# Group norm by half rows, and loads moved into and behind the turns of a scan, in a decoder block on one core

## The chip, the cores and the metric

The kernel runs on one core of one Trainium2 chip. The metric is the device time of one execution in microseconds (us); three runs were timed. All data are float32.

## The reference, cut to what matters

One decoder layer on 1024 tokens of width 1024. A combined input projection feeds a short convolution (512 channels) and an RWKV7 recurrence (8 heads of 64), both go through the output projection w_out, and then comes a mixture of experts, top 4 of 32.

```python
p = xn @ w_in
y_conv = c_b * causal_dwconv(c_c * c_h, conv_w)
...
y = rwkv7_scan(r, decay, k, v, -kk, kk * iclr)
mean = jnp.mean(y, axis=-1, keepdims=True)
var = jnp.mean(jnp.square(y - mean), axis=-1, keepdims=True)
y = (y - mean) * lax.rsqrt(var + GN_EPS) * ln_x_w + ln_x_b
y = y + jnp.sum(r * k * r_k, axis=-1, keepdims=True) * v      # the bonus
y_rwkv = y * g                                                # g = sigmoid(d_g) @ w_gate_up
h = x + jnp.concatenate([y_conv, y_rwkv], axis=-1) @ w_out
h = h + moe_ffn(rms_norm(h)); return rms_norm_final(h)
```

The scan's state, and with it y, is linear in v along the index over which the mean is taken (64 values of a head).

## The kernel before, in words

The kernel is written engine by engine (SP issues loads and stores, POOL is GpSimd, ACT ScalarE, DVE VectorE, PE TensorE), each with its own program, tied by semaphores that are waited for by hand. One large SBUF tensor, `arena`, holds nearly everything at fixed places (`at(kb, ...)`, kilobytes from its start), and places are reused from stage to stage. PSUM is one tensor `ps` of 8 banks.

Stages, with times of the profile: input projection and preparation of the scan's inputs `AR` (32 KB from 0), `BK` (32 KB from 32), `V` (from 64) up to about 375 us; convolution, in a loop over RT = 4 channel tiles, up to 412; the scan over NCH = 16 chunks of 64 tokens, two per turn of a loop (8 turns), up to 627; group norm, bonus and gate of y; output projection over TT = 8 token tiles, with residual, norm, router and lists between its halves, up to 795; then 32 experts, whose weights pass through six slots of 2 MB (`wslot`).

What a chunk needs is copied from AR, BK and V to small buffers: `stage` (lines 424, 425, 427) two chunks ahead, once PE has transposed the keys (`s_bt`), and `stage_again` (430) one chunk ahead, once Y is done (`s_y`). The helpers `chunk_half` on each engine name a chunk's steps. On PE, `m_product` (1534) comes one chunk early, `v_transposed` (1543) turns V by a product with the identity, `scores` (1550) begins a chunk's own part, `bk_transposed` (1561) waits for POOL's scaled keys (586); `e_`, `f_` and `ft_product` (1568, 1574, 1580) are the doubling steps of an inverse, `x`, `sa`, `state` and `y` products end it. The code of a turn is about 750 pairs of weight load and matmul. After the loop PE, ACT and DVE run one more half chunk (the drain), whose last step is ACT's copy of Y (832).

Each conv row tile goes to DRAM (`conv_d`, POOL 575) and POOL waits for it to land (577) before the next; the bonus rows went to DRAM earlier (`bonus_d`). After the last convolution row has landed, SP loads the four bonus tiles of 512 KB (437) and the gate weights (438), and then enters the scan's loop.

After the scan, per channel tile i (4 tiles of 128 channels by 1024 tokens), with `centre` = identity minus a block mean: PE `centred(i)` (1736), ACT `square` (867), PE `variance` (1747), ACT logarithm and exponential (881, 884), DVE scales (1207), adds bias and bonus (1212), PE `gate_of` (1754) and DVE multiplies by it (1215, 1216). All is double-buffered by whole tiles; the variance and gate banks are single:

```python
            variance(0)
            gate_of(0)
            for i in range(1, RT):
                variance(i)
                if i + 1 < RT:
                    centred(i + 1)
                gate_of(i)

            pe.wait_ge(s_wo, 16 * (RT + 4))
            pe.wait_ge(s_mix, RT)
```

Then `out_project(t, h)` (1773) multiplies token tile t by half h of w_out's columns, 8 products of 128x512: first the 4 of the convolution's channels, then the 4 of y's. A residual (DVE 1227, 1228), a square sum (ACT 915), a root and the scaled rows (DVE 1258) follow for each tile, and PE transposes them (1820) between the next tile's two halves. w_out's first half (455) is loaded at the end of the scan; the convolution rows (461), w_out's rest (462), constants (463, 464) and the first three expert weight slots (466) when the scan has ended; the router's inputs (468 to 470) and x (474) once the last gate product is done; the other three slots (502) when expert 0's tokens have been gathered.

## Time and profile before

| | us |
|---|---|
| three runs | 2333.19, 2338.95, 2339.39 (median 2338.95) |
| profiled execution, its own time | 2338.62 |
| its span, first to last instruction | 2337.1 |
| scan, first product to last Y copy | 412.19 to 626.62 |
| from there to the output projection's first product | 29.25 |
| mean granted clock of TensorE, share of full speed | 0.99 |

The profile lists, for one execution, each instruction with its start and duration, by engine and line. "Idle before" is the engine's idle time in front of an instruction, and "<-" names what released it; "issue" means that the profile shows nothing it waited for.
### The profile page before, as it was taken

The numbers are of one execution on the slowest core, as the hardware profiler recorded it, in microseconds if no ns is written. First come the engines' busy times: TensorE is split into PE (matmuls) and PEld (weight loads), VectorE is DVE, ScalarE is ACT, GpSimd is POOL, SyncE is SP. The second block draws the span as 40 slices with busy tenths as digits, with TensorE's granted clock in tenths as the row PEclk, the third lists the DMA queues.
The fourth block names the chain that finished last, engine by engine and source line by source line (L and its number), as shares of the span: only waits on it lengthen the run. The fifth ranks groups of instructions, "written<-read, shape, count | busy, mean of one in ns | idle before, by whom it ended". The sixth has DMA issues, their size and how long they took to land.

```text
span 2337.1 us, 46297 instructions
## 1 busy us (share of the span) xinstructions
PE 2283.6 (98%) x18286; PEld 1685.4 (72%) x18287; DVE 773.2 (33%) x1812; ACT 475.8 (20%) x979; POOL 343.8 (15%) x360
## 2 busy tenths in 40 slices
PE   8999999899999999999999999999999999999997
PEld 3444444799744678878887788878887788778875
DVE  6666411454434422222322222222222232223324
ACT  3223000344423211111111111111111111111113
POOL 0000000111102311111111111112111211112112
PEclk9999999999999899999999999999999999999999
DMA  3021111322443467977997779778897799668976
GB/s 139 27 76 40 54 45 54 107 70 78 165 186 110 183 230 276 351 289 266 334 350 283 276 297 344 283 282 315 296 349 276 285 334 350 266 252 333 350 301 255
DMA packets 111409, 534.97 MB, mean 229 GB/s; under 512 B 26771, under 2 KB 60711, under 8 KB 86752
## 3 DMA queue, kind: packets, MB, share of 16 engines
q1 hardware_dynamic: 89200, 489.30, 53.8%
q0 software_dynamic: 22160, 44.98, 7.6%
q8 instruction: 35, 0.57, 0.1%
q14 instruction: 14, 0.11, 0.0%
HBM read 485.24 MB, written 40.05 MB: 225 GB/s over the span
## 4 chain that ended last, share of the span: by engine, by line
PE 93%; DVE 3%; DMA 2%; issue 1%; ACT 1%; POOL 0%; SPq 0%; POOLq 0%; DVEq 0%; ACTq 0%
PE ps L1861 38%; PE ps L1881 18%; PE ps L1417 12%; PE ps L1773 5%; PE ps L1891 2%; PE ps L1870 2%; PE ps L1568 2%; PE ps L1580 2%; PE ps L1464 1%; PE ps L1574 1%; PE ps L1900 1%; DVE arena L1100 1%; PE ps L1550 1%; DMA idx_g<-list_s 1%; PE ps L1669 0%
## 5 line engine op out<-in xcount | busy, mean ns | idle before, releaser
L1861 PEld LDWEIGHTS ps<-arena 128*128 128x128 f32 x7808 | 925.9, 191 | 16.2 <-issue 15.2
L1861 PE MATMUL ps<-arena 128*128 128x128 f32 (+2 forms) x7808 | 926.9, 281 | 1.0 <-ACT arena L933 0.8
L1881 PE MATMUL ps<-arena 128*128 128x512 f32 x1024 | 453.3, 595 | 0.0
L1881 PEld LDWEIGHTS ps<-arena 128*128 128x128 f32 x1024 | 190.2, 190 | 221.3 <-issue 220.5
L1417 PE MATMUL ps<-arena 128*128 128x512 f32 x768 | 334.6, 595 | 0.8 <-ACT arena L739 0.8
L1314 DVE TENSOR_SCALAR arena<-ps,arena 128x160 f32<-128x160 f32 x256 | 98.3, 384 | 615.1 <-PE ps L1861 536.1
L1417 PEld LDWEIGHTS ps<-arena 128*128 128x128 f32 x768 | 146.0, 191 | 188.7 <-issue 188.7
L938 ACT ACTIVATE arena<-arena 128x160 f32<-128x160 f32 x256 | 86.1, 336 | 823.5 <-DVE arena L1314 823.5
L651 POOL DMA_INDIRECT sum_s<-arena,idx_s x31 | 51.5, 1662 | 819.6 <-ACT arena L953 819.6
L1773 PE MATMUL ps<-arena 128*128 128x512 f32 x256 | 112.8, 594 | 1.5 <-DVE arena L1216 1.5
L1318 DVE SCALAR_TENSOR_TENSOR arena<-arena 128x160 f32<-128x160 f32 x256 | 83.3, 325 | 49.7 <-ACT arena L938 49.7
L1315 DVE TENSOR_SCALAR arena<-ps,arena 128x160 f32<-128x160 f32 x256 | 96.2, 376 | 0.1
L635 POOL DMA_INDIRECT arena<-xn_s,idx_g x33 | 36.3, 1101 | 394.7 <-DMA idx_g<-list_s 204.5
L1335 DVE TENSOR_TENSOR arena<-ps,arena 128x512 f32<-128x512 f32 x31 | 21.4, 692 | 205.4 <-PE ps L1881 205.4
L1773 PEld LDWEIGHTS ps<-arena 128*128 128x128 f32 x256 | 47.5, 190 | 57.5 <-issue 57.5
L1321 DVE TENSOR_TENSOR arena<-arena 128x160 f32<-128x160 f32 x256 | 83.2, 325 | 8.8
L930 ACT COPY arena<-ps 128x512 f32<-128x512 f32 x66 | 35.4, 588 | 212.4 <-PE ps L1900 212.4
L1331 DVE TENSOR_TENSOR arena<-ps,arena 128x512 f32<-128x512 f32 x31 | 21.4, 692 | 161.6 <-PE ps L1881 161.6
L953 ACT ACTIVATE arena<-arena,idx_s 128x512 f32<-128x512 f32 x31 | 22.4, 722 | 202.1 <-DVE arena L1335 202.1
L1870 PE MATMUL ps<-arena 128*128 128x160 f32 x384 | 57.5, 299 | 2.7 <-issue 2.7
L1580 PE MATMUL ps<-arena 64*64 64x64 f32 x1328 | 54.3, 221 | 6.0 <-issue 5.4
L1870 PEld LDWEIGHTS ps<-arena 128*128 128x128 f32 x384 | 53.3, 190 | 2.9 <-issue 2.9
(265 smaller groups left out, 1849.0 us busy)
## 6 DMA issues: line engine op xcount, KB each, us to landing
arena<-gu_w SPq DMA_DIRECT2D x128, 2048.0 KB, 13.5
arena<-dn_w SPq DMA_DIRECT2D x64, 2048.0 KB, 14.1
arena<-dn_b SPq DMA_DIRECT2D x32, 512.0 KB, 16.2
arena<-w_in_t SPq DMA_DIRECT2D x26, 512.0 KB, 3.2
arena<-arena SPq DMA_DIRECT2D x50, 256.0 KB, 2.7
arena<-w_out SPq DMA_DIRECT2D x2, 2048.0 KB, 10.8
arena<-x SPq DMA_DIRECT2D x8, 512.0 KB, 5.3
xn_s<-arena SPq DMA_DIRECT2D x8, 512.0 KB, 2.6
```

The source lines that it names most:

```text
L651: pool.indirect_dma_start(acc_d, bass.IndirectOffsetOnAxis(ap=idx_s[:, 0:1], axis=0), Yt, None, compute_op=ALU.add).then_inc(s_sc, 16)
L938: nc.scalar.activation(sgm[f % 2], gt[f % 2], ACT.Sigmoid, scale=ALPHA).then_inc(s_gs, 1)
L1314: nc.vector.tensor_scalar(gt[b], ps[:, b, 0:C], g0, LIMIT, ALU.add, ALU.min).then_inc(s_g1, 1)
L1315: nc.vector.tensor_scalar(lt[b], ps[:, b, C:2 * C], g1, LIMIT + 1, ALU.add, ALU.min).then_inc(s_gd, 1)
L1318: nc.vector.scalar_tensor_tensor(out=lt[b], in0=lt[b], scalar=1 - LIMIT, in1=sgm[b], op0=ALU.max, op1=ALU.mult).then_inc(s_l1, 1)
L1321: nc.vector.tensor_tensor(actT[:, f, :], lt[b], gt[b], ALU.mult).then_inc(s_act, 1)
L1417: last = nc.tensor.matmul(ps[:, bank + h, :], win[:, slot, kt * P:(kt + 1) * P], xnT[:, kt, h * HALF:(h + 1) * HALF], start=kt == 0, stop= ...
L1580: last = nc.tensor.matmul(out_at(s, 1, h, r), Est[s][own(h), r, :], TTst[s][own(h), r, :], start=True, stop=True)
L1773: last = nc.tensor.matmul(ps[:, 2 * (t % 2) + h, :], mixT[:, k, t * P:(t + 1) * P], wo[:, k % RT, h * HALF:(h + 1) * HALF], start=k == 0, ...
L1861: last = nc.tensor.matmul(ps[:, f % 2, k * C:k * C + size], wslot[u][:, kt, o:o + P], xT[:, kt, 0:size], start=kt == 0, stop=kt == KT - 1, ...
L1870: last = nc.tensor.matmul(ps[:, 1, C:2 * C], wslot[3][:, kt, 3 * P:4 * P], xT[:, kt, :], start=False, stop=kt == KT - 1, skip_group_check= ...
L1881: last = nc.tensor.matmul(ps[:, 2 + h, :], actT[:, ft, 0:P], wslot[4 + h][:, ft, :], start=ft == 0, stop=ft == KT - 1)
```

## The change

1. The centring moves from y to v: `v_transposed` multiplies by blocks of `centre` instead of the identity, so that the scan gives y without its mean. The products `centred` go, and ACT and DVE read y from SBUF.
2. The norm is done by eight half tiles: q counts the first token half of the four channel tiles, then the second. Variance and gate products alternate between two banks each.
3. PE's order: the products of token tile 0 of the output projection stand between the variance and gate products; the convolution's part needs no y. Tiles 1 to 3 need only the first token half of y.
4. The bonus tiles are loaded at the end of the first four turns of the scan's loop, one each. POOL doesn't wait for the last convolution row.
5. In the last turn, once the last chunk's copies have landed, the convolution rows go to 32 KB (BK's place), w_out's rest to 53 KB, and the constants to theirs.
6. x's first tile is loaded ahead of the router's inputs; two expert weight slots follow behind x's second tile, and the third slot is loaded with the other three after the gathers.
7. ACT's table for logarithm and exponential is loaded before the scan's loop. PE waits for `centre` before its first product of the scan.

```diff
-        mixT = at(128, 2 * RT, T)
+        mix_conv, mix_y = at(32, RT, T), at(144, RT, T)
...
-        woA, woB = at(80, RT, D), at(176, RT, D)
+        woA, woB = at(80, RT, D), at(53, RT, D)
...
@@ SP
-            sp.wait_ge(s_cvr, RT + 1)
-            for i in range(RT):
-                sp.dma_start(bonus_in[:, i, :], bonus_d[i]).then_inc(s_pi, 16)
-            sp.dma_start(wgate, wgate_d).then_inc(s_pi, 16)
...
-            with sp.Fori(0, NCH // 2 - 1) as it:
+            def stage_turn(it):
                 stage_next(2 * it, 0, 2 * it + 2)
                 stage_next_again(2 * it, 1)
                 stage_next(2 * it + 1, 1, 2 * it + 3)
                 stage_next_again(2 * it + 1, 0)
+
+            with sp.Fori(0, RT) as it:
+                stage_turn(it)
+                sp.dma_start(bonus_in[:, bass.ds(it, 1), :].rearrange("p a t -> p (a t)"),
+                             bonus_d[bass.ds(it, 1)].rearrange("a p t -> (a p) t")).then_inc(s_pi, 16)
+            sp.dma_start(wgate, wgate_d).then_inc(s_pi, 16)
+            sp.wait_ge(s_cvo, 16 * RT)
+            with sp.Fori(RT, NCH // 2 - 1) as it:
+                stage_turn(it)
...
-            sp.wait_ge(s_yc, NCH + 2)
-            sp.wait_ge(s_cvr, RT + 1)
+            sp.wait_ge(s_st[0], 48 * (NCH // 2 + 1))
             for i in range(RT):
-                sp.dma_start(mixT[:, i, :], conv_d[i]).then_inc(s_wo, 16)
-            sp.dma_start(woB, w_out[RW:2 * RW, :].rearrange("(k p) n -> p k n", p=P)).then_inc(s_wo, 16)
...
-            for u in range(3):
-                sp.dma_start(wslot[u], weights_of(0, u)).then_inc(s_wt[u], 16)
+                sp.dma_start(mix_conv[:, i, :], conv_d[i]).then_inc(s_wo, 16)
+            sp.dma_start(woB, w_out[RW:2 * RW, :].rearrange("(k p) n -> p k n", p=P)).then_inc(s_par, 16)
...
             sp.wait_ge(s_gp, 2 * RT)
...
@@ POOL
-            with pool.Fori(0, RT) as i:
+            with pool.Fori(0, RT - 1) as i:
...
+            pool.wait_ge(s_cd, 2 * RT + 1)
+            pool.dma_start(conv_d[RT - 1], conv_st[:, 0, :]).then_inc(s_cvo, 16)
@@ ACT
+            def square(q):
+                i, h = q % RT, q // RT
+                nc.scalar.activation(gn_sq[q], YF[:, i, h * HALF:(h + 1) * HALF], ACT.Square).then_inc(s_ysq, 1)
...
@@ DVE
+            for q in range(2 * RT):
+                i, w = q % RT, slice(q // RT * HALF, (q // RT + 1) * HALF)
+                y = mix_y[:, i, w]
+                dve.wait_ge(s_sd, q + 1)
+                nc.vector.scalar_tensor_tensor(out=y, in0=YF[:, i, w], scalar=prm[:, LNW + i:LNW + i + 1], in1=gn_sd[q],
+                                               op0=ALU.mult, op1=ALU.mult).then_inc(s_nm, 1)
...
@@ PE
-                    last = nc.tensor.matmul(out_at(s, 3, 1 - h, r), Vc[s][own(h), r, :], cst[own(h), K_ID2:K_ID2 + L],
+                    last = nc.tensor.matmul(out_at(s, 3, 1 - h, r), Vc[s][own(h), r, :], centre[own(h), N * h:N * h + N],
                                             start=True, stop=True)
...
+            gate_of(0)
+            gate_of(1)
+            variance(0)
+            pe.wait_ge(s_wo, 16 * (RT + 1))
+            out_part(0, 0, 0, first)
+            variance(1)
+            out_part(0, 0, 0, second)
+            early_group(2)
+            out_part(0, 1, 0, first)
+            early_group(3)
+            out_part(0, 1, 0, second)
+            early_group(4)
+            pe.wait_ge(s_mix, RT)
+            pe.wait_ge(s_par, 2 * 16)
+            out_part(0, 0, 1).then_inc(s_op, 1)
+            early_group(5)
+            out_part(0, 1, 1).then_inc(s_op, 1)
+            early_group(6)
+            early_group(7)
```

(`early_group(q)` is the variance product of half tile q and then its gate product; `out_part(t, h, part, steps)` gives the products of one part of w_out's rows, 0 the convolution's and 1 y's.)

PE's order between the scan's last Y product (L1674) and the transposes of token tile 0 (L1820), before: L1736 is centring, L1747 variance, L1754 gate, L1773 output projection.

```order
L1736 MATMUL ps<-arena,centre 128x512 [waits centre_matrix,post_inputs,Y_copied]
L1736 MATMUL ps<-arena,centre 128x512 x3
L1747 MATMUL ps<-arena,cst 128x512 [waits y_squared] x2
L1754 MATMUL ps<-arena 128x512 x2
L1747 MATMUL ps<-arena,cst 128x512 [waits y_squared,var] x2
L1736 MATMUL ps<-arena,centre 128x512 [waits y_scaled_then_rstd]
```

After, the same place; L1742 is the gate, L1736 the variance, L1747 the output projection.

```order
L1742 MATMUL ps<-arena 128x512 [waits post_inputs,Y_copied]
L1742 MATMUL ps<-arena 128x512
L1736 MATMUL ps<-arena,cst 128x512 [waits y_squared]
L1747 MATMUL ps<-arena 128x512 [waits w_out_in]
L1747 MATMUL ps<-arena 128x512
L1736 MATMUL ps<-arena,cst 128x512 [waits y_squared]
L1747 MATMUL ps<-arena 128x512 x2
L1736 MATMUL ps<-arena,cst 128x512 [waits var,y_squared]
L1742 MATMUL ps<-arena 128x512 [waits mix_ready]
L1747 MATMUL ps<-arena 128x512 x2
```

The centring products are gone, and two products of the output projection stand between one variance product and the next; the pattern goes on to the eighth half tile.

SP's queue from the end of the scan's loop on, before:

```order
L455 DMA arena<-w_out 128x4x1024
L461 DMA arena<-conv_s 128x1024 [waits conv_stage_free,Y_copied]
L461 DMA arena<-conv_s 128x1024 x3
L462 DMA arena<-w_out 128x4x1024
L463 DMA cst<-consts 128x689
L464 DMA entry<-entry 128x320
L466 DMA arena<-gu_w 128x4096 x3
L468 DMA arena<-router_w 128x8x32 [waits gate_product]
L469 DMA arena<-router_b 128x32
L470 DMA arena<-normw 128x1024
L474 DMA arena<-x 128x1024 x2
```

And after:

```order
L459 DMA arena<-w_out 128x4x1024
L464 DMA arena<-conv_s 128x1024 [waits chunk_staged0]
L464 DMA arena<-conv_s 128x1024 x3
L465 DMA arena<-w_out 128x4x1024
L466 DMA cst<-consts 128x689
L467 DMA entry<-entry 128x320
L472 DMA arena<-x 128x1024 [waits gate_product]
L474 DMA arena<-normw 128x1024
L475 DMA arena<-router_w 128x8x32
L476 DMA arena<-router_b 128x32
L472 DMA arena<-x 128x1024
L479 DMA arena<-gu_w 128x4096 x2
```

The wait for the last Y copy is gone from the convolution rows, the expert weights stand behind x's second tile, and there are two of them.

## Rows read from the trace of the kernel before

**Rows 1.** The page: the chain that ended last, shares of the span by engine

```profile
PE 93%; DVE 3%; DMA 2%; issue 1%; ACT 1%; POOL 0%; SPq 0%; POOLq 0%; DVEq 0%; ACTq 0%
```

**Rows 2.** Busy us (PE, PEld, DVE, ACT, POOL) by stretch; then clock, DMA share, GB/s

```profile
412.00:436.00 24.00, 17.73 (x458) 16.94 (x462) 8.60 (x20) 6.57 (x18) 4.65 (x6) 0.86 0.48 160
460.00:484.00 24.00, 24.00 (x756) 23.08 (x754) 11.78 (x27) 11.68 (x32) 4.74 (x6) 1.00 0.28 77
416.00:424.00 8.00, 4.32 (x136) 4.05 (x132) 2.94 (x6) 2.55 (x8) 3.50 (x4) 1.00 0.85 291
426.00:432.00 6.00, 5.61 (x105) 5.61 (x107) 1.69 (x4) 1.48 (x4) 0.00 (x0) 0.50 0.07 20
626.00:650.00 24.00, 20.38 (x51) 8.02 (x47) 11.16 (x14) 15.71 (x22) 2.34 (x4) 1.00 0.95 367
```

**Rows 3.** PE in order of time, 412 to 462: start, duration, line, idle before

```profile
413.56 1.16 PE L1550 MATMUL ps<-arena 64*128 64x128 f32 x16
417.67 0.46 PE L1561 MATMUL ps<-cst,arena 64*128 64x64 f32 x8 [1.58 <-POOL arena L586]
426.39 0.48 PE L1580 MATMUL ps<-arena 64*64 64x64 f32 x4 [4.50 <-issue]
434.46 1.16 PE L1550 MATMUL ps<-arena 64*128 64x128 f32 x16
447.00 0.62 PE L1669 MATMUL ps<-arena 128*64 128x64 f32 x14 [1.05 <-issue]
449.07 1.16 PE L1550 MATMUL ps<-arena 64*128 64x128 f32 x16
461.06 1.16 PE L1550 MATMUL ps<-arena 64*128 64x128 f32 x16
```

**Rows 4.** All engines in order of time, 415 to 417

```profile
415.71 1.78 SPq L437 DMA_DIRECT2D arena<-bonus_s  x4
416.39 1.04 POOL L586 TENSOR_TENSOR arena<-arena,cL 128x512 f32<-128x512 f32 x1 [3.10 <-DMA conv_s<-arena]
```

**Rows 5.** Queue of instruction transfers, in 412:449 and in 461:485: packets, MB, share

```profile
q8 instruction: 5, 0.08, 0.9%
...
q8 instruction: 1, 0.02, 0.2%
```

**Rows 6.** DMA issues (whole run; x in 600 to 700): KB each, median us to landing

```profile
arena<-w_in_t SPq DMA_DIRECT2D x26, 512.0 KB, 3.2
...
arena<-x SPq DMA_DIRECT2D x4, 512.0 KB, 5.6
```

**Rows 7.** 626 to 656: groups by form (busy us, mean ns, idle before); first output product

```profile
L867 ACT ACTIVATE arena<-ps 128x512 f32<-128x512 f32 x8 | 4.8, 597 | 6.6 <-PE ps L1736 6.6
L881 ACT ACTIVATE arena<-ps,gneps 128x512 f32<-128x512 f32 x8 | 5.3, 686 | 1.3 <-PE ps L1747 1.2
L1207 DVE SCALAR_TENSOR_TENSOR arena<-ps,prm_sb,arena 128x512 f32<-128x512 f32 x8 | 5.6, 746 | 13.2 <-ACT arena L884 13.2
L1212 DVE SCALAR_TENSOR_TENSOR arena<-arena,prm_sb 128x1024 f32<-128x1024 f32 x4 | 5.1, 1285 | 0.1
...
655.87 0.67 PE L1773 MATMUL ps<-arena 128*128 128x512 f32 x1 [1.54 <-DVE arena L1216]
```

**Rows 8.** DVE and PE in order of time, 669 to 677

```profile
669.98 0.69 DVE L1227 TENSOR_TENSOR arena<-ps,arena 128x512 f32<-128x512 f32 x1 [13.89 <-PE ps L1773]
...
673.11 1.28 DVE L1258 SCALAR_TENSOR_TENSOR arena<-arena,stat 128x1024 f32<-128x1024 f32 x1
...
676.54 0.71 PE L1820 MATMUL ps<-cst,arena 128*128 128x128 f32 x5
```

**Rows 9.** SP's issues in order of time, 605

```profile
605.50 0.63 SPq L455 DMA_DIRECT2D arena<-w_out  x1
```

**Rows 10.** DVE in order of time in expert 0

```profile
815.72 0.38 DVE L1314 TENSOR_SCALAR arena<-ps,arena 128x160 f32<-128x160 f32 x1 [2.77 <-PE ps L1861]
820.07 0.38 DVE L1314 TENSOR_SCALAR arena<-ps,arena 128x160 f32<-128x160 f32 x1 [2.81 <-PE ps L1861]
```

173 lines of the change are left out of this document (75 added, 98 removed).

## The prediction

> **What bounds the kernel now.** I read the page's chain first: what ended last lies on TensorE (PE) for 93% of the span of 2337.1 us [rows 1]. So a change pays only where PE idles, where its granted clock falls to the lower level, or where it has fewer instructions. The profiled execution took 2338.62 us, 1.52 us more than its span; the median of the three runs is 2338.95 us, 0.33 us above the profiled one, so the sum below is made against 2338.62 and moved by nothing.
>
> The table of windows then shows two places. In the scan, a turn of two chunks takes 24 us with PE fully busy (460 to 484), but in 412 to 436 PE is busy 17.73 us of 24 at a clock of 0.86 [rows 2]. After the scan, in 626 to 650, it is busy 20.38 us of 24 with products of which a third will go [rows 2]. These are the two places that the change touches.
>
> **First turn of the scan.** The score products (L1550) of chunks 0, 1, 2 and 3 start at 413.56, 434.46, 449.07 and 461.06 [rows 3]. So chunk 0 takes 20.90 us, chunk 1 14.61, and from then on a chunk takes 11.99. The excess of chunk 0 is 8.91 us, and three pieces of it can be read [rows 3]. PE waited 1.58 us for POOL's L586, which itself had waited 3.10 us for the last convolution row to land in DRAM [rows 4]. PE stood 4.50 us at "issue", which means that nothing in the profile released it. Then it ran at a clock of 0.50, the 1.2 GHz level, in 426 to 432 [rows 2]: its products take twice their time there: 6 us of them at the lower level cost 3.0 us more than at the upper. Together 9.1, about the 8.91.
>
> The 4.50 us begin at 421.89. Over 416 to 424 the DMA engines are 85% busy [rows 2]: SP has issued the four bonus loads and the gate weights from 415.71 on [rows 4]. The queue of instruction transfers brings five packets in 412 to 449, but one in 461 to 485 [rows 5]. I take this as PE's code of the loop being fetched in its first turn, with one block late behind the bonus loads. In chunk 1, where no bonus load is in the way, the longest such stop is 1.05 us [rows 3].
>
> The change moves the bonus loads to the ends of turns 0 to 3, and POOL no longer waits for the last convolution row. Cost of chunk 0 after: I charge it what chunk 1 costs, 14.61 us, since it too fetches its code beside the staging copies alone. Both chunks then take 29.22 us instead of 35.51: a gain of 6.29. PE now also waits for the centre matrix before its first product, a DVE operation on 128x128 that stands behind the last convolution product as PE's did; a 512-column one takes 0.7 [rows 7], so I put it and its latency at 0.4 us, lost. **Net gain 5.9.** Bounds: if the late code has nothing to do with the loads, only POOL's 1.58 is won, 1.2 net. If chunk 0 has no stop at all it costs 11.99, net 8.5, and if chunk 1 too, 11.1. The row nearest to the case is chunk 1's own.
>
> Each bonus load is issued once per turn behind the copy for the next chunk (L430), and is 512 KB, like a tile of w_in, which lands in 3.2 us [rows 6]. The steady turns use 28% of the DMA engines [rows 2]: nothing added; if it did hold up a copy, that is the fourth rival. ScalarE's table load moves ahead of the scan, where ACT idles behind the convolution: nothing. The product with the centre matrix in V's transposition replaces one with the identity, same shape and count: nothing.
>
> **Between scan and output projection.** The last Y copy ends at 626.62 (the table above) and the output projection starts at 655.87 [rows 7]. In between PE executes 24 products of 128x512: 8 centring, 8 variance, 8 gate. Each costs 0.86 us of PE (24 of L1773 run from 655.87 to the transposes at 676.54 [rows 7, 8]: 20.67/24). That would be 20.6 us of 29.25; the rest is waiting. What ends last is a round through all three: ACT's squares waited 6.6 us for the centring products, and DVE's L1207 13.2 us for ACT's exponential [rows 7], and the next centring product waits for DVE.
>
> After the change the centring products are gone, and 16 of the 24 products that followed at L1773 (tile 0) are laid between the 8 variance and 8 gate products. PE's work from 626.67 to the transposes of tile 0 is thus 8 + 8 + 16 + 8 (tile 1, first half) = 40 products, 40 x 0.86 = 34.4 us, that is 661.1, if it never waits. Does it? Per half, ACT needs a square (0.60), a logarithm (0.69) and an exponential, which I put at the square's size, 0.62: 1.91. DVE needs L1207's 0.75, L1212 at half its 1.285 and some fixed part, 0.70, and a gate product of L1207's kind, 0.70: 2.15 [rows 7]. PE's spacing between variance products is 2.6 to 3.4 us (one of each kind and one or two pieces of the projection), up to 5.1 about the long pieces. So each is fed in time: first half-group scaled from 630.8, mixed at 633.0; the fourth mixed at 641.7, while PE wants it at 642.1; the last mixed at 657.5, which PE's first half of tile 1 doesn't need. I cost PE's waits there at nothing; the cover at the fourth is only 0.4 us.
>
> What is late next is tile 0's norm. DVE can add the residual from 657.5, but x's rows are issued only when the last gate product is done, at 654.3 (before, it was wanted at 669.98 only [rows 8]). A 512 KB load lands 3.2 us (w_in_t) to 5.6 us (x, with others in the queue) after issue [rows 6]: 657.5 to 659.9. From the residual's start to the scaled rows it takes 669.98 to 674.39 [rows 8], 4.41 us: 661.9 to 664.3, with the router's inputs landing at about the same time. I take 663.1 for the transposes, 2 us after PE arrives. Before they started at 676.54 [rows 8]. **Gain 13.4**, with 15.4 (no wait) and 12.2 as ends. After it, PE's order is as before, since each tile costs it the same.
>
> **Loads.** The convolution rows, the second half of w_out and the constants (4.6 MB) move from 626.64 to about 606, behind w_out's first half, issued at 605.50 [rows 9]. At the 367 GB/s of 626 to 650 [rows 2] all 6.7 MB take 18 us: in by 624, before PE wants them at 628. No expert weights compete at 630. The third weight slot is loaded after the gathers instead, at about 801 in the old time. Expert 0 uses up a slot in 8.7 us (DVE reads two results of PE per slot, 4.35 us apart [rows 10]), from some 807 on. Four slots of 2 MB need 5.7 us each at 367 GB/s: the third is in by 808 and wanted at 824, the last by 825 and wanted past 840. Nothing added; if the cover went, some 5 us.
>
> **Sum.** 2338.62 - 5.9 - 13.4 = **2319.3 us**. With every low end of gain 2325.2, with every high end 2312.1.
>
> **Where a page differs.** The Trainium skill, "Runtime: NRT & Kernel Launch", section "Instruction fetch mechanics", says that crossing a code block costs one DMA tail-bump, "mostly hidden". The stops of 1.05 and 4.50 us speak against it [rows 3]; by the rule the 4.50 has another cause and stays, which is the first rival below. The same section calls the instruction memory "only 2 cache lines", with which a loop of this length would be fetched anew in each turn; that is the fourth rival, and the single packet of a later turn speaks against it [rows 5].
>
> **Rivals.**
> - *The late code has another cause* (the entry into the loop, not the loads). For it: the profile names no releaser. Against: the DMA load just then, and stops of only 1 us elsewhere. Gain 1.2 instead of 5.9: 2324.0 us. Chance 0.12.
> - *The new burst delays code at the scan's end.* The loads now fill the DMA engines from 606 to 624, while PE leaves its loop for code it has not run. Against: by then much of it may be there, since the drain is short. Price, as in chunk 0: 4.5 of waiting and 3.0 of lower clock, 2326.8. Chance 0.12.
> - *The half-groups run in series.* If a semaphore's latency adds 0.5 us to each ACT and DVE step, the fourth group comes late, and the four groups behind it wait about 1.2 us each: 2324. Chance 0.12.
> - *The other side: code is fetched in every turn.* Then each of the four bonus loads stops PE as the burst did in chunk 0, 4.5 + 3.0 = 7.5 us, 30 in all, and the time is 2349.3, slower by 0.4%. It decides from 6.6 us per turn on (above 2345.6). For it: the loop's code is long. Against: one packet in 461 to 485 where the first turn had five [rows 5]. Chance 0.02.
> - *The change does less than it says* because router inputs or x's rows come still later (they now share the queue with 4 MB of expert weights issued behind them): each us is a us. 3 to 5 us, 2323. Chance 0.12.
>
> **Numbers.** The forecast has 0.50. The range 2312 to 2329 takes in the bounds of the sum and the values of the first, second, third and fifth rival (2323 to 2326.8), and leaves out the fourth and two mishaps at once. A measurement of this kernel can tell about 0.3%, 7.0 us. All but the other side and a pile of mishaps lie below 2331.9: faster 0.94, same 0.03, slower 0.03.
>
> **What would show it.** Right: L1550 of chunk 1 some 15 us after chunk 0's, and a clock near 1.00 in the first turn; bonus loads between chunks with no gap of PE beside them; no wait of POOL for the last convolution row's transfer; PE without an idle piece over 0.5 us from the last Y copy to the end of tile 1's first half; transposes of tile 0 some 36.5 us after that copy (before 49.9); a wait of about 2 us there for the scaled rows. Wrong: a gap at "issue" in the drain, a clock below 1 in the 30 us after the scan, DVE as releaser of the gate products, or gaps ahead of expert 0's fifth gate product.

## The result, and the profile after

| | before | after |
|---|---|---|
| median of the runs, us | 2338.12 (4 runs, 2333.19 to 2339.39) | 2319.47 (4 runs, 2315.90 to 2321.75) |
| profiled execution, us | 2338.62 | 2320.9 |
| its span, us | 2337.1 | 2319.3 |
| mean granted clock | 0.990 | 0.992 |
| first product of the scan (L1534) starts | 412.19 | 412.31 |
| last copy of Y (L832, now L839) ends | 626.62 | 621.50 |
| transposes of tile 0 (L1820, now L1827) start | 676.54 | 657.62 |

The ratio is 0.9925 with an interval of 0.9911 to 0.9938: three quarters of a per cent faster, or 17.5 us of 2338.12 (the medians differ by 18.65 us). The forecast was 2319.3 us.

The share of the chain by engine hardly moves (against [rows 1]), as it must where the time was taken out of pauses:

```profile
PE 94%; DVE 3%; DMA 2%; issue 1%; ACT 0%; POOL 0%; SPq 0%; POOLq 0%; DVEq 0%; ACTq 0%
```

Busy time by stretch, with the columns of [rows 2]. The first three are the scan's first turn, the two chunks after it and a steady turn; then the last turn with the new burst of loads, and the 24 us from the last copy of Y on:

```profile
412.00:436.00 24.00, 21.75 (x649) 20.44 (x651) 11.29 (x25) 9.84 (x27) 6.31 (x8) 1.00 0.31 90
436.00:460.00 24.00, 22.40 (x643) 21.18 (x639) 10.96 (x24) 9.83 (x27) 3.46 (x5) 0.93 0.24 72
460.00:484.00 24.00, 24.00 (x758) 23.08 (x754) 11.81 (x27) 11.70 (x32) 4.68 (x7) 1.00 0.35 99
600.00:624.00 24.00, 21.65 (x584) 19.09 (x581) 7.64 (x17) 10.17 (x27) 2.95 (x5) 1.00 0.77 297
621.50:645.50 24.00, 23.95 (x56) 10.74 (x57) 13.14 (x18) 12.19 (x20) 2.35 (x4) 1.00 0.08 29
```

In 412 to 436 PE is busy 21.75 us at clock 1.00, where it was 17.73 us at 0.86. From 621.50 on it is busy 23.95 of 24 us, where it was 20.38 of 24 [rows 2].

PE in order of time in the first three chunks, as in [rows 3]: the start of the scan, the score products (L1550) that mark each chunk, and every idle piece at "issue":

```profile
412.31 0.68 PE L1534 MATMUL ps<-arena 64*64 64x64 f32 x16 [1.26 <-DVE arena L1132]
413.69 1.16 PE L1550 MATMUL ps<-arena 64*128 64x128 f32 x16
420.64 0.33 PE L1580 MATMUL ps<-arena 64*64 64x64 f32 x4 [0.21 <-issue]
424.88 0.45 PE L1669 MATMUL ps<-arena 128*64 128x64 f32 x8 [0.15 <-issue]
426.64 1.16 PE L1550 MATMUL ps<-arena 64*128 64x128 f32 x16
430.10 0.34 PE L1561 MATMUL ps<-cst,arena 64*128 64x64 f32 x5 [0.67 <-issue]
434.99 0.50 PE L1580 MATMUL ps<-arena 64*64 64x64 f32 x9 [0.91 <-issue]
440.62 0.62 PE L1669 MATMUL ps<-arena 128*64 128x64 f32 x14 [1.60 <-issue]
443.12 2.08 PE L1550 MATMUL ps<-arena 64*128 64x128 f32 x16
456.06 1.16 PE L1550 MATMUL ps<-arena 64*128 64x128 f32 x16
```

Chunk 0 takes 12.95 us (it took 20.90), chunk 1 16.48 (14.61), chunk 2 12.94 (11.99). The stop of 4.50 us is now 0.21 us, in front of the same four records of L1580 (a float32 product has two records, each with a weight load of its own). Chunk 1 has longer stops than before, and chunk 2 begins at the lower clock: the 16 records of its score products take 2.08 us, not 1.16, and 436 to 460 has 0.93. The three chunks together shrink from 47.50 to 42.37 us.

POOL in order of time at the scan's start. It issues the last convolution row's copy to DRAM and works on (L593 was L586, which had waited 3.10 us [rows 4]):

```profile
412.07 0.53 POOL L584 DMA_DIRECT2D conv_s<-arena  x1 [40.29 <-DVE arena L1132]
412.71 1.06 POOL L593 TENSOR_TENSOR arena<-arena,cL 128x512 f32<-128x512 f32 x1
```

The groups of the norm by form in 621.5 to 657, which answer to [rows 7] (square, logarithm, exponential on ACT; the scaling on DVE). ACT still waits for PE's variance products, and DVE for ACT, but PE no longer waits for either:

```profile
L874 ACT ACTIVATE arena<-arena 128x512 f32<-128x512 f32 x8 | 4.8, 617 | 0.0
L886 ACT ACTIVATE arena<-ps,gneps 128x512 f32<-128x512 f32 x8 | 5.5, 688 | 13.3 <-PE ps L1736 13.3
L888 ACT ACTIVATE arena<-arena 128x512 f32<-128x512 f32 x8 | 5.1, 632 | 0.3
L1210 DVE SCALAR_TENSOR_TENSOR arena<-arena,prm_sb 128x512 f32<-128x512 f32 x8 | 6.0, 751 | 14.4 <-ACT arena L888 14.4
```

The end of the stretch in order of time on SP, DVE and PE: x's rows, the residual, the scaled rows, the transposes (against [rows 8]):

```profile
649.32 0.35 SPq L472 DMA_DIRECT2D arena<-x  x1
...
653.15 0.69 DVE L1224 TENSOR_TENSOR arena<-ps,arena 128x512 f32<-128x512 f32 x1 [0.27 <-DMA arena<-x]
...
656.28 1.28 DVE L1255 SCALAR_TENSOR_TENSOR arena<-arena,stat 128x1024 f32<-128x1024 f32 x1
...
657.62 1.09 PE L1827 MATMUL ps<-cst,arena 128*128 128x128 f32 x8 [1.46 <-DVE arena L1255]
```

From the last copy of Y to these transposes it was 49.92 us and is 36.12. So the account is: 5.1 us won up to the last copy of Y (626.62 to 621.50), 13.8 after it, 1.1 given back later (tile 0's transposes to the end: 1660.6 us before, 1661.7 after). Together 17.8, the difference of the two spans. The 5.1 us are one execution against one; below, the other executions spread this part widely.

What is given back is found in expert 0. Its first product starts 18.86 us earlier than before (787.75 for 806.61). Then PE in order of time, at the first down projection, before and after:

```profile
842.72 1.89 PE L1870 MATMUL ps<-arena 128*128 128x160 f32 x12 [2.69 <-issue]
```

```profile
823.89 3.38 PE L1877 MATMUL ps<-arena 128*128 128x160 f32 x12 [2.73 <-issue]
```

The stop at "issue" was there before, at the same twelve records, and it is no longer than it was. Behind it they now take 3.38 us instead of 1.89: 1.5 us for the lower clock (820 to 832 has 0.86, where 838 to 850 had 1.00). About 0.4 us of that is regained behind it.

### The profile page after: what moved, and what is told of

It is laid out like the page before. It is cut to its first block, busy times and chain, and to the rows that moved or that the text cites. A ratio compares the mean times of both kernels' runs of the same rounds, so it can differ in the third digit from the quotient of the medians.

```text
span 2319.3 us, 46282 instructions
## 1 busy us (share of the span) xinstructions
PE 2273.4 (98%) x18270; PEld 1682.5 (73%) x18271; DVE 774.8 (33%) x1816; ACT 477.6 (21%) x983; POOL 344.3 (15%) x360
## 4 chain that ended last, share of the span: by engine, by line
PE 94%; DVE 3%; DMA 2%; issue 1%; ACT 0%; POOL 0%; SPq 0%; POOLq 0%; DVEq 0%; ACTq 0%
PE ps L1868 39%; PE ps L1888 19%; PE ps L1417 13%; PE ps L1747 4%; PE ps L1898 2%; PE ps L1877 2%; PE ps L1568 2%; PE ps L1580 2%; PE ps L1464 1%; PE ps L1574 1%; PE ps L1907 1%; DVE arena L1104 1%; PE ps L1550 1%; DMA idx_g<-list_s 1%; PE ps L1669 0%
## 5 line engine op out<-in xcount | busy, mean ns | idle before, releaser
L1868 PEld LDWEIGHTS ps<-arena 128*128 128x128 f32 x7808 | 925.9, 191 | 17.4 <-issue 15.3
L1747 PE MATMUL ps<-arena 128*128 128x512 f32 x256 | 113.7, 594 | 0.0
L1747 PEld LDWEIGHTS ps<-arena 128*128 128x128 f32 x256 | 47.6, 190 | 55.2 <-issue 54.7
L1580 PE MATMUL ps<-arena 64*64 64x64 f32 x1328 | 53.3, 218 | 1.7 <-issue 1.1
## 6 DMA issues: line engine op xcount, KB each, us to landing
arena<-gu_w SPq DMA_DIRECT2D x128, 2048.0 KB, 12.1
arena<-dn_w SPq DMA_DIRECT2D x64, 2048.0 KB, 14.5
```

What stands on the lines that cost most here:

```text
L1580: last = nc.tensor.matmul(out_at(s, 1, h, r), Est[s][own(h), r, :], TTst[s][own(h), r, :], start=True, stop=True)
L1747: last = nc.tensor.matmul(ps[:, 2 * (t % 2) + h, :], (mix_conv, mix_y)[part][:, k, t * P:(t + 1) * P], (woA, woB)[part][:, k, h * HALF:(h ...
L1868: last = nc.tensor.matmul(ps[:, f % 2, k * C:k * C + size], wslot[u][:, kt, o:o + P], xT[:, kt, 0:size], start=kt == 0, stop=kt == KT - 1, ...
```

## The experiments

Two questions. In the first turn: is it the loads, POOL's wait or the code itself that stopped PE? Behind the scan: which of the three edits (centring moved, halves, early products of tile 0) is worth how much? My theories were those of the prediction. Each variant's own profiled execution is read by two lengths: the first three chunks (from one score product to the third after it), and "tail", from the last chunk's transposing products (L1561 in before and after) to tile 0's transposes. "First packet" is when, to 0.2 us and counted from the scan's first product, the queue of instruction transfers moves its first packet of 16 KB.

| kernel | chunks 0, 1, 2, us | sum | first packet, us | stop at the four records of L1580 | tail, us |
|---|---|---|---|---|---|
| before | 20.90, 14.61, 11.99 | 47.50 | 11.6 | 4.50 | 68.45 |
| c_centre_only | 17.72, 15.95, 11.99 | 45.66 | 9.8 | 3.00 | 65.70 |
| c_first_turn_as_before | 17.36, 15.22, 11.99 | 44.57 | 9.2 | 2.60 | 54.52 |
| b_bonus_in_turns | 15.40, 16.41, 12.99 | 44.80 | 7.2 | 0.81 | 69.52 |
| a_bonus_ahead | 15.65, 14.68, 11.99 | 42.32 | 7.8 | 2.09 | 54.61 |
| a_pool_waits | 14.14, 15.50, 11.99 | 41.63 | 7.0 | 0.26 | 54.60 |
| the change | 12.95, 16.48, 12.94 | 42.37 | 6.0 | 0.21 | 54.66 |
| the change again (d_change) | 12.39, 15.48, 11.99 | 39.86 | 4.8 | none | 54.49 |
| c_groups_first | 12.34, 15.71, 11.99 | 40.04 | 4.8 | none | 57.66 |
| c_last_groups_early | 12.12, 15.70, 11.99 | 39.81 | 4.8 | none | 53.65 |
| d_last_groups_early | 12.95, 16.22, 12.90 | 42.07 | 5.4 | 0.21 | 53.66 |
| a_late_loads | 12.62, 14.67, 11.99 | 39.28 | 4.8 | none | 64.76 |
| d_extra_loads | 12.93, 16.77, 12.90 | 42.60 | 4.8 | none | 54.46 |
| d_code_shift_96 | 13.54, 12.80, 11.99 | 38.33 | 3.6 | none | 54.77 |

Three profiles have the first turn as before (before, c_centre_only, c_first_turn_as_before): their sums have a mean of 45.91 us. Six have that of the change and no other edit in the scan: their mean is 40.57, from 39.28 to 42.37. So the first turn is worth 5.3 us by the means, and single pairs give 2.2 to 8.2.

### The loads ahead of the loop, and GpSimd's wait

**a_bonus_ahead**, the change with its loads put back:

```diff
-            with sp.Fori(0, RT) as it:
-                stage_turn(it)
-                sp.dma_start(bonus_in[:, bass.ds(it, 1), :].rearrange("p a t -> p (a t)"),
-                             bonus_d[bass.ds(it, 1)].rearrange("a p t -> (a p) t")).then_inc(s_pi, 16)
+            sp.wait_ge(s_cvo, 16 * RT)
+            for i in range(RT):
+                sp.dma_start(bonus_in[:, i, :], bonus_d[i]).then_inc(s_pi, 16)
             sp.dma_start(wgate, wgate_d).then_inc(s_pi, 16)
-            sp.wait_ge(s_cvo, 16 * RT)
-            with sp.Fori(RT, NCH // 2 - 1) as it:
+            with sp.Fori(0, NCH // 2 - 1) as it:
                 stage_turn(it)
```

> The changed kernel with one thing undone: the four bonus tiles and the gate weights are loaded ahead of the scan's loop again. Theory (PE's code of the first turn comes late behind these loads): a stop of PE of 3 to 5 us at "issue" at the same product as in the kernel before (L1580 with 4 of 16 records left), some us at the lower clock behind it, chunk 0 (score product to score product) at 18 to 20 us instead of 12.95, the kernel some 5 to 7 us slower than the changed one, that is 13 us faster than before. Rival (the stop comes with the entry into the loop, and went for another reason, such as POOL's wait): chunk 0 stays at 13 us and the time at that of the changed kernel.

Measured: 2320.36 us, ratio 0.9936 [0.9920, 0.9953]. The stop in front of the same four records is back, at 2.09 us, with the DMA engines 74% busy around it:

```profile
422.59 0.33 PE L1578 MATMUL ps<-arena 64*64 64x64 f32 x4 [2.09 <-issue]
```

```profile
412.00:424.00 12.00, 9.52 (x288) 9.09 (x290) 5.84 (x12) 3.99 (x11) 3.91 (x5) 1.00 0.74 257
```

But the clock stays at 1.00. The three chunks sum to 42.32 us, 1.75 more than the mean of the change's first turn and no more than its longest (42.37), so by themselves the loads cost under half of what I had charged them. My 18 to 20 us for chunk 0 and my 5 to 7 us in the time were both too much.

**a_pool_waits**, the change with GpSimd waiting for the last convolution row again:

```diff
-            with pool.Fori(0, RT - 1) as i:
+            with pool.Fori(0, RT) as i:
...
-            pool.wait_ge(s_cd, 2 * RT + 1)
-            pool.dma_start(conv_d[RT - 1], conv_st[:, 0, :]).then_inc(s_cvo, 16)
```

> The changed kernel with one thing undone: POOL waits for the last convolution row to land before it starts on the scan. If that wait was worth its 1.58 us, chunk 0 takes 14.5 us instead of 12.95 and PE's first transposition of keys (L1561) waits for POOL's L593. If the code's arrival sets chunk 0's pace anyway, the wait takes the place of a stop at "issue" and chunks 0 and 1 together stay at 29.4 us.

One execution: 2318.1 us. PE waits 1.13 us for GpSimd and chunk 0 is 14.14 us, near the 14.5 I expected if the wait is a cost of its own; the sum of the three chunks lies between the change's own two executions.

**b_bonus_in_turns**, the kernel before with the new loop of loads alone:

> The kernel before with one part of the change: the bonus tiles are loaded at the ends of turns 0 to 3 of the scan's loop; POOL still waits for the last convolution row. Theory: the stop of 4.50 us and the spell at the lower clock go, the scan ends 3.5 to 5 us earlier, and nothing else moves, so 2334 us. Rival (entry into the loop): the stop stays, 2338 us.

Measured: 2330.36 us, ratio 0.9978 [0.9968, 0.9988]. The 4.50 us stop is 0.81 us and GpSimd's 1.57 us remain. This is 2.7 us less over three chunks than in the profile of before (1.1 less than the mean of the three such profiles), and 0.22% or 5.1 us by the ratio. The spell at the lower clock did not go, as I had expected, but moved to chunk 2. Its tail is 1.1 us longer than before's, because the first output products run at the lower clock:

```profile
650.90:656.30 5.40, 5.38 (x9) 2.45 (x10) 0.24 (x3) 0.00 (x0) 0.00 (x0) 0.69 1.02 373
```

There before's products had the clock at 1.00 (655.80 to 661.20).

**c_first_turn_as_before** puts both back into the change, that is, both diffs above:

> The changed kernel with both edits of the first turn undone: the bonus and gate loads stand ahead of the loop again, and GpSimd waits for the last convolution row ahead of the loop. What stays is the part behind the scan. Theory (the stop of 4.50 us in before needs the loads, and each of the two undone alone cost nothing because their sum has to pass a point at which the granted clock falls): chunk 0 is 20 to 21 us again, clock 0.8 to 0.9 in the first 24 us, the scan 4 to 6 us longer than in the changed kernel, 2323.5 to 2326. Rival (the 4.5 us stop was a matter of where the code of before's stages stands, or of chance): chunk 0 stays at 14 to 16 us and the time within 1 us of the changed kernel's 2319.5.

Measured: 2323.11 us, ratio 0.9940 [0.9924, 0.9957]. Beside 0.9925 and 0.9921 for the change that is 3.5 to 4.4 us, though the intervals overlap. PE in order of time, the two idle pieces of chunk 0:

```profile
413.26 0.47 PE L1557 MATMUL ps<-cst,arena 64*128 64x64 f32 x8 [1.09 <-POOL arena L589]
...
420.09 0.48 PE L1576 MATMUL ps<-arena 64*64 64x64 f32 x4 [2.60 <-issue]
420.36 1.08 PE L1564 MATMUL ps<-arena 64*64 64x64 f32 x16
```

Behind the stop sixteen records take 1.08 us where they take 0.63 at the upper level: the lower clock is back, as in before. So chunk 0 reads: both edits made 12.1 to 13.0 us (13.5 in d_code_shift_96, which starts at the lower clock), GpSimd's wait alone 14.1 and 15.4, the loads alone 15.7, both 17.4 to 20.9. The four profiles with the loads ahead have the stop at 2.09 to 4.50 us, and the ten without at 0 to 0.81: the loads set its size. In three of those four GpSimd's wait is there too, and in those three PE then ran for a while at the lower clock; with the loads alone it did not. My expectation of 20 to 21 us for chunk 0 was too high, here and in c_centre_only: before's own profiled execution, from which I took it, had the longest stop of the three.

### Where the stops lie: code or data

**d_code_shift_96**, the change with 96 more instructions on PE ahead of the loop:

```diff
             pe.addr_align(FETCH_BLOCK, max_nops=0)
+            for _ in range(96):
+                pe.sem_inc(s_pe_apart, 1)
```

> The changed kernel with 96 extra instructions (increments of a semaphore that nobody reads) in TensorE's program ahead of the scan's loop. Theory (the stops at issue are places at which the next piece of the program is not there yet, and lie at fixed distances in the program): the stops move against the code by 96 instructions, which are 48 products with their weight loads, so three groups of 16 products earlier: the stop at the 9th-last product of L1580 and that at the 14th-last of L1669 are gone from there and stand some 1.5 to 3 us earlier in the chunk, at other lines. Rival (the stops belong to a data or semaphore event, or to the loop's own branch): they stay at L1580 and L1669, with the same counts of products behind them. The time stays within 3 us of the changed kernel.

One execution: 2321.04 us. Chunk 1 in order of time, first of d_change, then of the shifted kernel (whose lines stand two further down, so that L1655 is L1653):

```profile
432.59 0.68 PE L1653 MATMUL ps<-arena 64*64 64x64 f32 x16
433.06 0.68 PE L1580 MATMUL ps<-arena 64*64 64x64 f32 x16
433.53 0.68 PE L1659 MATMUL ps<-arena 64*64 64x64 f32 x16
434.14 0.33 PE L1669 MATMUL ps<-arena 128*64 128x64 f32 x2
435.52 0.62 PE L1669 MATMUL ps<-arena 128*64 128x64 f32 x14 [1.05 <-issue]
```

```profile
439.56 0.28 PE L1655 MATMUL ps<-arena 64*64 64x64 f32 x3
440.34 0.57 PE L1655 MATMUL ps<-arena 64*64 64x64 f32 x13 [0.51 <-issue]
440.74 0.63 PE L1582 MATMUL ps<-arena 64*64 64x64 f32 x16
441.20 0.63 PE L1661 MATMUL ps<-arena 64*64 64x64 f32 x16
441.77 0.69 PE L1671 MATMUL ps<-arena 128*64 128x64 f32 x16
```

The stop stood behind the second record of L1669; now it stands behind the third of L1655. In between lie 13 + 16 + 16 + 2 = 47 records, or 94 instructions with their weight loads, for 96 that were added. The stop belongs to a place in the program, not to a semaphore or a tile. The run has a price of its own: the added instructions run while PE has nothing else, its first product waits 7.71 us and starts at the lower clock, 2.8 us later than in the change's profile; the other stops of the first turn are gone. In one execution I can't tell which of that is the earlier start of fetching.

The other thirteen profiles say the same without any shift. They have 46 stops at "issue" behind the first product of the scan, and each lies at one of five places: behind 244, 368, 491, 615 or 738 records of the scan, which are 123 or 124 records apart (the stop of the shifted kernel lies behind 691, which is 738 less 47). And the instructions can be seen to arrive: in all fourteen, each stop ends 2.3 to 3.4 us after a packet of the queue of instruction transfers has started. For the stop at L1580 with the loads ahead this packet comes 7.8 to 11.6 us after the scan's first product, and the stop ends 2.4 to 2.7 us behind it; without them it comes after 3.6 to 7.2. So the loads make the code late, and late code is what PE stands still for.

**d_extra_loads**, the change with a burst of four loads in each of turns 0 to 3:

```diff
-            with sp.Fori(0, RT) as it:
+            for k in range(2):
+                sp.wait_ge(s_bo[k], 16 * RT // 2)
+            for it in range(RT):
                 stage_turn(it)
...
+                sp.dma_start(bonus_in[:, it, :], bonus_d[it]).then_inc(s_pi, 16)
+                for k in range(3):
+                    sp.dma_start(at(84 + 4 * k, T), x[0:P, :]).then_inc(s_extra, 16)
+                sp.wait_ge(s_extra, 48 * it + 48)
```

> The changed kernel with three more loads of 512 KB (rows of x, into a part of the memory that is free there) behind the bonus load in each of turns 0 to 3, so that each of these turns has a burst of four loads, as before had once ahead of the loop. Theory (code of the loop is fetched in the first turn only): the bursts of turns 1 to 3 stop TensorE nowhere, chunks take 11.99 us each there; only the burst of turn 0, if it meets chunk 1's fetch, can lengthen a stop; 2319 to 2324. Rival 4 of the prediction (code is fetched in every turn): a stop at issue of 2 to 4.5 us in each of the turns 1 to 3 and in part the lower clock, 2326 to 2340.

One execution: 2321.53 us. The turns with bursts 1 and 2 by windows (columns as above):

```profile
460.00:484.00 24.00, 24.00 (x756) 23.08 (x754) 11.88 (x26) 11.61 (x33) 4.67 (x7) 1.00 0.51 165
484.00:508.00 24.00, 24.00 (x758) 23.09 (x754) 11.89 (x26) 11.59 (x33) 4.74 (x6) 1.00 0.51 164
```

The DMA engines are nearly twice as busy as in [rows 2], and PE has no idle piece from 460 to 532, behind the bursts of turns 1 to 3. The queue of instruction transfers moves its last packet of the loop before 484, in this run as in before and after. The loop's code is fetched once.

### The stretch behind the scan

**c_centre_only**, the kernel before without the eight centring products (the transposing copy takes its centred form from the centre matrix, as in the change; groups stay whole tiles):

```diff
-                    last = nc.tensor.matmul(out_at(s, 3, 1 - h, r), Vc[s][own(h), r, :], cst[own(h), K_ID2:K_ID2 + L],
+                    last = nc.tensor.matmul(out_at(s, 3, 1 - h, r), Vc[s][own(h), r, :], centre[own(h), N * h:N * h + N],
...
-                if i + 1 < RT:
-                    centred(i + 1)
```

> The kernel before, changed only in where Y is centred: the eight centring products after the scan go, and the transposing copy of each chunk takes its centred form from the centre matrix; tiles stay whole, the first product of tile 0 still stands behind all groups, loads and first turn stay as before. Theory (the 13.8 us gained after the scan are partly the removal of 8 products of 1024 columns in two halves each, about 7 us of PE time in a chain of rounds): the groups' rounds get shorter by what the centring took in them, 3 to 7 us; time 2328 to 2332 where before is 2335. Rival (the rounds are bound by the chain square, product, Ln, Exp, scale, whole tile, and the centring lay in its gaps): under 1.5 us. The first turn must stay at about 20.9 us for its first chunk in both.

Measured: 2333.93 us, ratio 0.9984 [0.9973, 0.9994]; tail 65.70 us, 2.75 less than before, between my two ranges. PE in order of time, and ahead of it the first thing that ACT does there:

```profile
620.84 1.28 ACT L869 ACT_TABLE_LOAD   x1
...
622.90 1.96 PE L1737 MATMUL ps<-arena,cst 128*128 128x512 f32 x4 [2.49 <-ACT arena L866]
...
630.89 2.99 PE L1744 MATMUL ps<-arena 128*128 128x512 f32 x4 [2.60 <-DVE arena L1216]
...
642.25 3.53 PE L1744 MATMUL ps<-arena 128*128 128x512 f32 x4 [2.52 <-DVE arena L1216]
```

Eight products of 0.86 us are gone, 6.9 us of PE, and only 2.75 us come out: PE now waits in their place, and some products behind a wait run at the lower clock (2.99 and 3.53 us for four records, 1.88 at the upper level; before had one such group, of 3.50). Part of the first wait is ACT's table load of 1.28 us, which the centring products had covered and which the change moves ahead of the scan. So this run understates the centring's part by up to that much.

**c_groups_first**, the change with tile 0's sixteen early products behind the groups instead of between them:

```diff
+            variance(1)
+            for q in range(2, 2 * RT):
+                early_group(q)
             pe.wait_ge(s_wo, 16 * (RT + 1))
             out_part(0, 0, 0, first)
-            variance(1)
             out_part(0, 0, 0, second)
-            early_group(2)
...
             out_part(0, 0, 1).then_inc(s_op, 1)
-            early_group(5)
+            out_part(0, 1, 0, first)
+            out_part(0, 1, 0, second)
             out_part(0, 1, 1).then_inc(s_op, 1)
-            early_group(6)
-            early_group(7)
```

> The changed kernel with TensorE's 16 early products of tile 0 behind the norm's groups instead of between them (half groups, centring in the scan and all loads stay as changed). Theory (the early products fill the gaps of the half groups' rounds): tile 0's transposes come about 4 us later, and the time is 2322 to 2325 where the changed kernel has 2319.5. Rival (the rounds are bound by the chain through ScalarE and VectorE, so that the order on TensorE is worth little, and a plain order lets them run closer together): under 1.5 us later. Sign the other way: the groups end earlier by 3 us or more because their products no longer queue behind output products, and the net is zero.

Measured: 2318.95 us, ratio 0.9922 [0.9906, 0.9939]; tail 57.66 us, 3.0 more than the change. The 2322 to 2325 that I expected did not come. Rounds of half groups in order of time, with PE's waits in them:

```profile
620.37 1.12 PE L1736 MATMUL ps<-arena,cst 128*128 128x512 f32 x2 [1.10 <-ACT arena L874]
622.22 1.12 PE L1742 MATMUL ps<-arena 128*128 128x512 f32 x2 [0.73 <-DVE arena L1216]
...
624.39 1.12 PE L1742 MATMUL ps<-arena 128*128 128x512 f32 x2 [0.19 <-DVE arena L1216]
```

Even without anything between them, half groups run at a round of 2.17 us, of which PE waits 0.19 us: DVE's three steps and PE's two products nearly match. So, taken in this order, 2.75 us of the tail's 13.8 come with the centring, 8.0 with the halves and everything else that changed between the two runs (65.70 to 57.66: the moved loads, the table load of 1.28 us), and 3.0 with the early products. All but 0.1 of the 8.0 us lie ahead of the first output product, and PE, ACT and DVE wait for no load there in either run; still, the halves alone have no run of their own. The whole time does not show the 3.0: the change itself was not run on that chip, and the interval spans 7.7 us. The kernel below is 3.2 us faster on that chip, where the tails differ by 4.0.

**c_last_groups_early** and **d_last_groups_early** are one kernel, the change with the last two half groups ahead of tile 0's last eight products:

```diff
             early_group(5)
-            out_part(0, 1, 1).then_inc(s_op, 1)
             early_group(6)
             early_group(7)
+            out_part(0, 1, 1).then_inc(s_op, 1)
```

> The changed kernel with the last two half groups' products put ahead of the last 8 early products of tile 0. Theory (in the changed kernel the transposes of tile 0 wait 1.46 us for VectorE, which is late because it mixes the last half groups late): that wait goes and the transposes come 0.5 to 1.5 us earlier; 2318 to 2319 where the changed kernel has 2319.5, at the edge of what can be told. Rival (VectorE's work up to the residual of tile 0 is fixed by the x load that lands at 653.15, or the last 8 products now stand at the end and are themselves the last link): no gain, within 0.5 us, or up to 1 us lost.

> The changed kernel itself, run beside the variants on one chip, so that they can be compared with it directly. All theories: ratio to before 0.991 to 0.994. By the theory that the size of the stops in the first turn differs from execution to execution, but not their place, the profiled execution stops at the same products of L1580 (x4, x9) and L1669 (x8, x14) as before, with sizes between 0 and 1.7 us, and the part from the last scan chunk's transposition to tile 0's transposes takes 54.6 us again.

> The changed kernel with the last two half groups' products ahead of the last 8 early products of tile 0, now with more rounds beside the changed kernel. Theory: 53.65 us from the last scan chunk's transposition to tile 0's transposes where the changed kernel has 54.66, so 1.0 us less in the whole, 2315 to 2319 where the changed kernel has 2316 to 2320. Rival (the 1.0 us is given back in the experts, whose start is fixed by something else): no difference within 0.5 us.

d_change came out as expected: its ratio is 0.9921, its tail 54.49 us, and its stops (0.39 to 1.17 us) lie at L1580 x9, at L1669 x14 and, not on my list, at L1561 x5, where the change's first profile had one of 0.67. For the variant, the tail is 53.65 and 53.66 us where the change has 54.66 and 54.49, and PE no longer waits for the scaled rows. The time shows nothing of it: 2315.78 us with a ratio of 0.9903 [0.9886, 0.9919] on one chip, 2316.93 with 0.9924 [0.9911, 0.9938] on another, where the change itself ran at 2313.43 and 0.9921 [0.9907, 0.9934]. Whether the 0.9 us is real in the whole stays open; no version here is shown to beat the change.

### The loads of the last turn

**a_late_loads**, the change with the convolution rows, the second half of w_out and the constants behind the last copy of Y again:

```diff
+            sp.wait_ge(s_yc, NCH + 2)
```

> The changed kernel with one thing undone: the convolution rows, the rest of w_out and the constants are issued when the scan has ended. Theory (the early burst is what lets tile 0's products be laid between the norm's): PE waits for the fourth convolution row ahead of the first product of the output projection, wanted 2.7 us after the last Y copy; issued by 1.8 us and 6 us to land, that is a wait of about 5 us, the rest of w_out coming in its cover, so 4 to 6 us slower than the changed kernel. Rival (the early burst costs as much in late code or contention as it gives): no slower. Expected here: PE's drain between the last loop turn and the last Y copy is as long as in the changed kernel, within 0.3 us.

Measured: 2325.99 us, ratio 0.9962 [0.9948, 0.9977], so about 8.6 us behind the change's 0.9925. PE in order of time:

```profile
630.26 3.62 PE L1748 MATMUL ps<-arena 128*128 128x512 f32 x4 [8.37 <-DMA arena<-conv_s]
```

The early products need the convolution rows at 621.9 and get them at 630.3; then four records take 3.62 us at the lower clock, not 1.88. Both together are the 10.1 us by which the tail grows. I had expected 4 to 6: the slowest of the four rows took 9.8 us from issue to landing, not 6, and the lower clock was not in my sum. From the last chunk's transposing products to the last copy of Y it is 18.53 us here, 18.54 in the change and 18.53 before, so the early burst costs the scan's end nothing. The early products can't do without it; what the moved loads are worth without early products, no run shows.

## Why the prediction was right, and where its parts were off

**Start of the scan.** I charged 0.4 us for the wait for the centre matrix, and it is there: PE idles 1.26 us ahead of the scan's first product, released by DVE, where it idled 0.83 before, so 0.43 us. That this product started only 0.12 us later than before (412.31 for 412.19) is chance, since its start differs by up to 4.6 us between executions for a reason ahead of the scan (last section).

**First turn, 5.9 us (1.2 to 11.1).** The profile of the change gives 5.1 us over three chunks and d_change 7.6, and the means over all profiles 5.3; the step holds. That the first pair came so near to the forecast is in part luck, as the spread of 2.2 to 8.2 shows. Its parts were placed differently. I took chunk 0 at 14.61 us and it was 12.1 to 13.0; I took chunk 1 as unchanged at 14.61 and it was 14.7 to 16.5, as if the delay moved on to where code and the chunks' own copies met (argued, not shown). Chunk 2 at the lower clock (0.95 us more), which four of the fourteen profiles have, I had not considered. The reading that the stop is code held back by the bonus loads is shown from three sides: its place moves with the program (d_code_shift_96), its size with the loads (2.09 to 4.50 us with them ahead, 0 to 0.81 without), and the packet of instructions ahead of its end comes late with the loads (7.8 to 11.6 us after the scan's first product, 3.6 to 7.2 without them).

**The late code has another cause (2324.0).** This falls: the 4.50 us went, and the stops that are left in the change's profile are 0.15 to 1.60 us each. By the Trainium skill, "Runtime: NRT & Kernel Launch", section "Instruction fetch mechanics", a crossing is "mostly hidden". The traces of this first turn disagree (0.15 to 1.60 us each).

**From the scan to tile 0's transposes, 13.4 us (12.2 to 15.4).** Measured 13.8. PE's 40 products without a wait were right: it is busy for 34.60 of the 34.66 us. The fourth half group, whose cover I had put at 0.4 us, was ready at 636.72 and wanted at 637.11. I had PE at the transposes 34.4 us after the copy of Y and it arrived after 34.7 (657.62 less the wait of 1.46). I took x's load at 3.2 to 5.6 us and it took 3.8, from 649.32 to the residual at 653.15, so the wait for the scaled rows was 1.46 us, not 2. What the forecast didn't say, and the variants show, is that the larger part of this comes with the halves (8.0 us, with the moved table load in it), and that the removed centring products, a third of PE's work there, are worth 2.75 us by themselves.

**Loads, nothing.** In 600 to 624 the DMA engines are 77% busy, and the drain is as long as before (18.54 and 18.53 us to the last copy of Y). Its only "issue" piece is 0.51 us; before's own profile lacks it, but b_bonus_in_turns and c_centre_only have it too, whose loads come behind the scan. The second rival (2326.8) falls. But "nothing added" at expert 0 was wrong by about 1 us. I looked there for a product that waits for its weights, and there is none. The price is at a stop at "issue" in the expert's first pass: between the first two profiles only the lower clock behind it (1.5 us), in most others the stop itself too. In the three profiles with the old loads of expert weights (before, b_bonus_in_turns, c_centre_only) it is 2.18 to 2.72 us; in the eleven with two slots loaded ahead and four in a burst behind the gathers it is 2.50 to 3.85, with a mean of 3.36, and in nine of them the twelve records behind it run in part at the lower clock (2.67 to 3.55 us instead of 1.89), as in one of the three (2.19). The stop is late code here too: in all fourteen it ends 2.6 to 2.8 us after the start of an instruction packet, and in the 4 us ahead of it the DMA engines are full (shares of 0.93 and more). That the burst of four slots makes it longer is argued and not shown, since no run here moved those loads alone.

**Half groups in series (2324).** This falls too: their round is 2.17 us, and PE waits 0.19 us of it at most once running.

**The other side (2349.3).** Four loads in a burst in turns 1 to 3 cost nothing, so code is not fetched in every turn. The prediction took "only 2 cache lines" for TensorE too, and that was misread: the same section of the Trainium skill gives the two lines for a memory of 32 KiB, and 128 KiB or 2048 instructions for TensorE. A turn's 750 pairs are about 1500 instructions, so by that figure they fit (an estimate), and d_extra_loads agrees.

**x or router inputs late (2323).** The wait for x was 0.27 us.

**Not in the sum:** the 1.1 us given back behind tile 0's transposes, by the lower clock in expert 0 above. Over the eleven profiles of the change and its variants this last part of the kernel takes 1660.1 to 1662.2 us, with a mean of 1661.1, and in the three with the old loads 1659.9 to 1660.6, with a mean of 1660.1. The forecast's 19.3 us of gain were 18.9 in the spans up to tile 0's transposes; the 2319.3 met the median of 2319.47 within the noise, and so closely by luck.

## What to carry to other kernels

The first pass through a long loop is where its code arrives: keep bulk loads out of it and put them, one per turn, into the turns behind; look for the same at every later loop that is entered under a burst of loads. Where products wait in a chain through two other engines, taking products out turns in large part into waiting (6.9 us of products gave 2.75 here); the larger gain came with halving the pieces. Before you shorten a stretch, look at what its inputs need: early work without early loads cost 8.4 us of waiting and some lower clock.

## What the runs showed that I had not expected

A stop can bring the lower clock on top of its own length, or not. In chunk 0, GpSimd's 1.1 to 1.6 us and a stop of 2.6 to 4.5 us brought the lower level with them; a stop of 2.09 us alone did not (412 to 436 stays at 1.00 in a_bonus_ahead). Which of the two makes the difference, the length of the stop or GpSimd's wait, no run separates.

Executions differ by 4 to 5 us for a reason that lies ahead of the change. Windows 100:200 and 200:300, of before and then of d_change, whose code is the same there:

```profile
100.00:200.00 100.00, 95.20 (x215) 40.34 (x214) 63.12 (x81) 29.52 (x38) 1.87 (x3) 0.98 0.16 57
200.00:300.00 100.00, 96.83 (x220) 41.62 (x219) 54.03 (x57) 16.06 (x21) 4.90 (x4) 0.98 0.13 47
```

```profile
100.00:200.00 100.00, 95.20 (x219) 40.54 (x218) 64.84 (x80) 29.18 (x37) 1.88 (x3) 1.00 0.16 57
200.00:300.00 100.00, 96.83 (x224) 41.78 (x223) 51.45 (x57) 16.65 (x22) 4.90 (x4) 1.00 0.15 52
```

PE is equally busy in both, but the clock granted is 0.98 in one and 1.00 in the other, and the scan's first product starts at 412.19 or at 408.34. One and the same kernel shows both: c_last_groups_early has 0.98 and starts its scan at 412.58, d_last_groups_early has 1.00 and starts at 409.06. So single executions can be compared stage by stage, from a mark inside the stage, but their whole times only to some 5 us. That is also why the halves of this change could be priced from the traces, and an improvement of 0.9 us could not be told in the time.
